# Seven-product form in more weight groups of a two-layer attention and recurrence trunk on one Trainium2 core, with the weight sums added by DMA

## What is computed

```python
for l in range(DEPTH):
    h = _rmsnorm(x, norm_gain[l])
    proj = jnp.einsum('bsd,de->bse', h, w_in[l])
    q, k, v, g_attn, x_rnn, g_rnn = jnp.split(proj, splits, axis=-1)
    attn = _swa_sink_attention(q, k, v, sinks[l], cos, sin)
    xc = _causal_conv(x_rnn, conv_w[l], conv_b[l])
    rnn = _rg_lru(xc, w_rgate[l], b_rgate[l], w_igate[l], b_igate[l], lru_param[l])
    mixed = jnp.concatenate([attn * jax.nn.silu(g_attn), rnn * jax.nn.silu(g_rnn)], axis=-1)
    x = x + jnp.einsum('bse,ed->bsd', mixed, w_out[l])
return _rmsnorm(x, final_gain)
```

## Time and profile before

| | us |
|---|---|
| median of 3 runs | 2312.78 (2311.39 to 2314.31) |
| the profiled execution | 2313.38 |
| its span in the profile | 2311.6 |
| PE busy | 2296.4 (99%) |
| DVE busy | 1637.6 (71%) |
| ACT busy | 1330.1 (58%) |
| read from memory | 244.48 MB |

### The profile page before, as it was taken

The page is one execution under the profiler, slowest core; times in us unless marked ns, Lnnn a source line. Parts: engine busy times, 40 slices in busy tenths (PEclk is TensorE's granted clock), DMA queues, the critical chain, the costliest instruction groups (busy, mean ns, idle before and its releaser), DMA issues.

```text
span 2311.6 us, 36747 instructions
## 1 busy us (share of the span) xinstructions
PE 2296.4 (99%) x13690; PEld 1915.2 (83%) x13690; DVE 1637.6 (71%) x2767; ACT 1330.1 (58%) x2551; POOL 0.8 (0%) x10
## 2 busy tenths in 40 slices
PE   9999999999999999999999999999999999999999
PEld 8888888898888888888888888888888888888888
DVE  7568778766547877867675786787765478777775
ACT  7558666434456767644565676763354557666444
POOL 0000000000000000000000000000000000000000
PEclk9999999999999999999999999999999999999999
DMA  5334333434333233344435433233343333333344
GB/s 194 103 109 139 95 89 92 117 113 123 95 99 88 85 99 85 99 143 117 148 96 157 164 105 93 89 97 115 116 119 97 95 95 89 89 90 100 110 119 151
DMA packets 138563, 255.28 MB, mean 110 GB/s; under 512 B 15632, under 2 KB 30224, under 8 KB 137616
## 3 DMA queue, kind: packets, MB, share of 16 engines
q1 hardware_dynamic: 137808, 252.77, 36.6%
q10 hardware_dynamic: 576, 0.16, 0.0%
HBM read 244.48 MB, written 8.39 MB: 109 GB/s over the span
## 4 chain that ended last, share of the span: by engine, by line
PE 85%; DVE 8%; DMA 4%; issue 2%; ACT 2%; SPq 0%; DVEq 0%; ACTq 0%; POOL 0%; POOLq 0%
PE proj L508 75%; DMA wraw<-in_w 3%; PE proj L527 2%; DVE wcut L1140 2%; PE proj L541 2%; PE ps_at L621 1%; PE ps_at L646 1%; PE ps_at L665 1%; PE proj L557 1%; DVE x L1443 1%; ACT wcut L750 1%; DVE room L1154 1%; DVE wraw L1155 1%; DVE wraw L1156 1%; DVE room L1158 0%
## 5 line engine op out<-in xcount | busy, mean ns | idle before, releaser
L508 PE MATMUL proj<-operand,wcut 128*128 128x512 f32 x8520 | 1973.2, 391 | 0.3 <-DVE proj L1203 0.3
L508 PEld LDWEIGHTS proj<-operand,wcut 128*128 128x128 f32 x8520 | 1591.4, 188 | 343.9 <-issue 11.2
L750 ACT ACTIVATE wcut<-wraw 128x512 fp32r<-128x512 f32 x803 | 505.6, 630 | 768.4 <-PE proj L508 657.3
L1140 DVE TENSOR_TENSOR wcut<-wraw,wcut 128x512 fp32r<-128x512 f32 x804 | 553.6, 689 | 522.5 <-ACT wcut L750 517.7
L527 PE MATMUL proj<-xsum,wcut 128*128 128x256 f32 x720 | 99.4, 283 | 0.0
L527 PEld LDWEIGHTS proj<-xsum,wcut 128*128 128x128 f32 x720 | 92.1, 192 | 0.0
L907 ACT ACTIVATE room<-ps_at,stat 128x128 f32<-128x128 f32 x256 | 90.0, 363 | 0.8
L855 ACT ACTIVATE gy<-proj 32x512 f32<-32x512 f32 x144 | 85.0, 590 | 3.8
L760 ACT ACTIVATE crosscut<-room 128x384 fp32r<-128x384 f32 x80 | 42.0, 526 | 54.5 <-DMA room<-in_w 26.5
L541 PE MATMUL proj<-operand,crosscut 128*128 128x256 f32 x480 | 70.5, 283 | 0.0
L541 PEld LDWEIGHTS proj<-operand,crosscut 128*128 128x128 f32 x480 | 64.3, 192 | 1.2
(11 more groups left out here) (181 smaller groups left out, 1810.0 us busy)
## 6 DMA issues: line engine op xcount, KB each, us to landing
wraw<-in_w SPq DMA_DIRECT2D x804, 256.0 KB, 2.6
room<-in_w SPq DMA_DIRECT2D x80, 128.0 KB, 2.7
x<-in_xt SPq DMA_DIRECT2D x2, 4096.0 KB, 13.7
mixed<-in_xt SPq DMA_DIRECT2D x14, 512.0 KB, 7.1
gw<-in_gates SPq DMA_DIRECT2D x32, 128.0 KB, 2.7
out<-x SPq DMA_DIRECT2D x4, 1024.0 KB, 4.9
out<-mixed SPq DMA_DIRECT2D x7, 512.0 KB, 3.2
tab<-in_cossin SPq DMA_DIRECT2D x8, 256.0 KB, 3.5
```

The source lines that it names most:

```text
L508: last = pe.matmul(bank[:, :], wcut[:, u % RING, a, c:c + P], operand[:, k, b, :], start=(k == 0 and n == 0), stop=(k == KT - 1 and n == 2 ...
L750: act.activation(wcut[:, u % RING, 0, :], wraw[:, u % RING, :], ACT.Copy).then_inc(w_hi, 1)
L1140: dve.tensor_tensor(wcut[:, u % RING, 1, :], wraw[:, u % RING, :], wcut[:, u % RING, 0, :].bitcast(F32), ALU.subtract).then_inc(w_lo, 1)
```

## The change

The seven-product form is used in more groups: 12 to 15 of the input projection and 19 to 24 of the output projection in every pass (19 to 23 in the last), and 4 to 6 in the passes of layer 2. That is 10, 13, 10 and 12 groups in the four passes, where 5 in each were before.

The order of the products is new. A group in this form has four whole units and seven half units: each half unit is one of the seven products for all four pairs (12 matmuls of 256 columns), with a weight tile of 256 KB of its own. Four of them (`lead`) run in the slots of the group before, three (`late`) in the group's own slots. `beats_of` says which units a slot holds: none, one or two. ACT and DVE cut the tile of a slot's first unit at its start and that of the second at its end. The wait for the banks' evacuation stands before the last matmul of the unit ahead.

The weight sums S1 to S4 are made by POOL's DMAs in device memory, copies and accumulating transfers from a second copy of the weights (`blocks`), 12 batches of one or two groups, during the first half of the tokens; the second half reads them again. `weight_sums`, `cross_part` and `crosscut` are gone.

The token sums of the input projection are computed by DVE into the room of `x`. For that, `x` is stored to device memory in slots 1 to 4 of layer 2 (four transfers of 1 MB), and in both layers it is loaded again at slot 125 (`RELOAD`), after the last half unit of group 15; the reload at slot 60 is gone. In layer 1 the output stores free the room.

Queries are evacuated at 0 and 2 slots after their group, and the second tile of an xr group after 2 slots instead of 6. The tables' second load moves from slot 196 to 70, the identity's load to the end.

```diff
+IN_LAST = 15
+EARLY_SEVEN = {(0, 0): (), (0, 1): (4, 5, 6), (1, 0): (), (1, 1): (4, 5, 6)}
+SEVEN = {(h, l): (*EARLY_SEVEN[h, l], *range(12, IN_LAST + 1),
+                  *range(PG + 2, PG + (7 if (h, l) == (LAST, DEPTH - 1) else 8)))
+         for h in range(HALVES) for l in range(DEPTH)}
+NPAIR = 4
+JS = {"in": (0, 1, 4, 5), "out": (0, 1, 2, 3)}
+LEAD = ((0, 0, 0, None), (1, 0, 1, 1), (3, 1, 1, 0), (2, 1, 0, 2))
+LATE_OF = ((4, 0, 0, None), (5, 0, 1, None), (6, 1, 0, 3))
+A11, S2, S3, S1, A12, S4, A22, A21 = range(8)
+WHOLE = {A11: 0, A12: 1, A21: 2, A22: 3}
+SUMS = {S1: 0, S3: 1, S2: 2, S4: 3}
...
+def beats_of(h, l, g):
+    mine, ahead = g in SEVEN[h, l], g + 1 in SEVEN[h, l]
+    p = [("plain", g, j) for j in range(UPG) if not mine or j not in JS[zone_of(g)]]
+    a = [("lead", g + 1, b) for b in range(4)]
+    t = [("late", g, b) for b in range(3)]
+    if mine and ahead:
+        return [t[:2], p[:1], p[1:2], t[2:], a[:2], a[2:], p[2:3], p[3:]]
+    if mine:
+        return [t[:1], t[1:2], p[:1], t[2:], p[1:2], [], p[2:3], p[3:]]
+    if ahead:
+        return [p[:1], p[1:2], p[2:3], [p[3], a[0]], [p[4], a[1]], [p[5], a[2]], a[3:], p[6:]]
+    return [[n] for n in p]
...
-Q_EV = 16
+Q_AT = [2 * UPG + UPG * (t // 2) + 2 * (t % 2) for t in range(AT)]
...
-XR_EV = [slot_of("xr", j) + 6 * (j % 2) for j in range(RT)]
+XR_EV = [slot_of("xr", j) + 2 * (j % 2) for j in range(RT)]
...
-TAB_LD = 196
+TAB_LD = 70
+T_AT = {(h, l, "out"): (126, 128, 136, 143) for h in range(HALVES) for l in range(DEPTH)}
+T_AT.update({(0, 0, "in"): (24, 26, 28, 30), (0, 1, "in"): (6, 7, 9, 11), (1, 0, "in"): (25, 33, 41, 49),
+             (1, 1, "in"): (6, 7, 9, 11)})
+SPILL = (1, 3, 0, 2)
+SPILL_AT = 1
+RELOAD = UPG * IN_LAST + 5
...
+                        for u in BEAT[h, l, s]:
+                            next_u = u + RING if u + RING < TOTAL else u + RING - UPG
+                            kind, g, j = UNIT[next_u][2:]
+                            what = {"lead": LEAD, "late": LATE_OF}[kind][j][0] if kind != "plain" else None
+                            sp_.wait_ge(w_lo, u + 1)
+                            if h == 0 and what in SUMS:
+                                sp_.wait_ge(built[what], 32 * (batch_of(UNIT[next_u][1], g) + 1))
+                            sp_.dma_start(wraw[:, u % RING, :], source(next_u)).then_inc(w_in[u % RING], 16)
...
+                        if l == 1 and s - SPILL_AT in range(4):
+                            i = SPILL[s - SPILL_AT]
+                            sp_.wait_ge(evac, at_evac(h, 0, tile_of("o", 4 * i + 3)))
+                            sp_.dma_start(x_kept[i], x[:, 4 * i:4 * i + 4, :].rearrange("p k t -> p (k t)")
+                                          ).then_inc(kept[i], 16)
+                        if s == RELOAD:
+                            sp_.wait_ge(unit_done, TURNED[h, l, "in"])
+                            if l == 0:
+                                sp_.dma_start(x[:, :, :], xt[h]).then_inc(xres_in, 16)
+                            else:
+                                sp_.dma_start(x[:, :, :].rearrange("p (i k) t -> p i (k t)", i=4),
+                                              x_kept.rearrange("i p c -> p i c")).then_inc(xres_in, 16)
...
+            def copy(to, batch, what):
+                l, g, size = BATCH[batch]
+                src = (blocks[WHOLE[what], l, g:g + size] if what in WHOLE else sums[SUMS[what], l, g:g + size])
+                pool.dma_start(sums[SUMS[to], l, g:g + size].rearrange("g r e -> (g r) e"),
+                               src.rearrange("g r e -> (g r) e")).then_inc(built[to], 16)
+            def add(to, batch, what):
+                l, g, size = BATCH[batch]
+                pool.dma_start(sums[SUMS[to], l, g:g + size].rearrange("g r e -> (g r) e"),
+                               blocks[WHOLE[what], l, g:g + size].rearrange("g r e -> (g r) e"),
+                               accum_op=ALU.add, max_dma_last_dim=4 * 4 * TOK).then_inc(built[to], 16)
+            pool.wait_ge(unit_done, START_SUMS)
+            for n in range(len(BATCH) + 1):
+                now, before = n < len(BATCH), n > 0
+                if before:
+                    copy(S4, n - 1, S2)
+                if now:
+                    copy(S1, n, A21)
+                    copy(S3, n, A11)
+                    pool.wait_ge(built[S1], 32 * n + 16)
+                    add(S1, n, A22)
+                    pool.wait_ge(built[S3], 32 * n + 16)
+                    add(S3, n, A21)
+                if before:
+                    pool.wait_ge(built[S4], 32 * n - 16)
+                    add(S4, n - 1, A12)
+                if now:
+                    pool.wait_ge(built[S3], 32 * n + 32)
+                    copy(S2, n, S3)
+                    pool.wait_ge(built[S2], 32 * n + 16)
+                    add(S2, n, A22)
+                    pool.wait_ge(built[S2], 32 * n + 32)
+                    pool.wait_ge(built[S1], 32 * n + 32)
+                if before:
+                    pool.wait_ge(built[S4], 32 * n)
...
+            def next_bank(n):
+                h, l, kind, g, j = UNIT[n]
+                if n > 0 and UNIT[n - 1][:2] == (h, l) and j == 0 and (kind == "lead" or (kind == "plain" and
+                                                                                     g not in SEVEN[h, l])):
+                    pe.wait_ge(evac, h * (DEPTH * TILES) + (l * TILES + 2 * g + 2))
...
+            def halved(n):
+                h, l, kind, g, j = UNIT[n]
+                zone = zone_of(g)
+                what, m, half, t = (LEAD if kind == "lead" else LATE_OF)[j]
+                if t is not None and g == next(i for i in SEVEN[h, l] if zone_of(i) == zone):
+                    pe.wait_ge(xsum_lo, at_t(h, l, zone, NPAIR - 1))
+                for i, pair in enumerate(JS[zone]):
+                    for p, (a, b) in enumerate(((0, 0), (0, 1), (1, 0))):
+                        if t is None:
+                            src = operand[:, KU * pair + (kind == "late"), b, HT * half:HT * half + HT]
+                        else:
+                            src = xsum[zone][i][:, HI_PART[zone][i] ^ b, t, :]
+                        if (i, p) == (NPAIR - 1, 2):
+                            next_bank(n + 1)
+                        last = pe.matmul(bank_of(l, 2 * g + m)[:, HT * half:HT * half + HT],
+                                         wcut[:, n % RING, a, P * i:P * i + P], src,
+                                         start=(kind == "lead" and j % 2 == 0 and (i, p) == (0, 0)),
+                                         stop=(kind == "lead" and (i, p) == (NPAIR - 1, 2)), skip_group_check=True)
...
+                act.activation(lead_u[:, :], bank_of(l, 2 * g)[:, 0:HT], ACT.Copy).then_inc(lead_copy, 1)
+            def lead_copy_back(h, l, g):
+                n = LED.index((h, l, g))
+                act.wait_ge(lead_done, 3 * n + 3)
+                act.activation(bank_of(l, 2 * g + 1)[:, 0:HT], lead_v[:, :], ACT.Copy).then_inc(lead_back, 1)
...
-            def weight_sums(h, l, g, i):
...
+                    mark(dve.tensor_tensor(to[0], first[:, 0:HT], first[:, HT:TOK], ALU.subtract))
+                    mark(dve.tensor_scalar(to[0], to[0], g1, None, ALU.mult))
+                    mark(dve.scalar_tensor_tensor(to[1], second[:, HT:TOK], g2, to[0], ALU.mult, ALU.add))
+                    mark(dve.scalar_tensor_tensor(to[2], first[:, 0:HT], g1, to[1], ALU.mult, ALU.subtract))
+                    dve.scalar_tensor_tensor(to[3], second[:, 0:HT], g2, to[1], ALU.mult,
+                                             ALU.subtract).then_inc(xsum_done, 1)
...
+                dve.wait_ge(unit_done, LED_AT[3][n])
+                dve.wait_ge(lead_half, n + 1)
+                if n > 0:
+                    dve.wait_ge(lead_back, n)
+                dve.tensor_tensor(first[:, HT:TOK], second[:, HT:TOK], lead_u[:, :], ALU.add).then_inc(lead_done, 1)
+                dve.tensor_tensor(lead_v[:, :], second[:, 0:HT], lead_u[:, :], ALU.subtract).then_inc(lead_done, 1)
+                dve.wait_ge(lead_done, 3 * n + 2)
+                dve.tensor_tensor(second[:, HT:TOK], lead_v[:, :], second[:, HT:TOK], ALU.subtract).then_inc(lead_done, 1)
...
+                        for u in BEAT[h, l, s][1:]:
+                            if u + AHEAD < TOTAL:
+                                weight_lo(u + AHEAD)
+                                dve.wait_ge(w_lo, u + AHEAD + 1)
```

474 lines of the change are left out of this document (231 added, 243 removed).

## The result

The change makes the kernel slower: 2374.74 us (2365.05 to 2376.78, four runs) against 2313.55 us, a ratio of 1.0257 with a 95% interval of 1.0242 to 1.0272. The profiled execution has a span of 2375.0 us, 63.4 us more than before's 2311.6. The forecast of 2350 had the sign and the main mechanism, but 24.7 us too little, and the time lies 2.7 us above the range. The four executions took 2376.8, 2376.8, 2372.7 and 2365.1 us, at mean granted clocks of PE of 0.989, 0.990, 0.992 and 0.995; before's are within 3 us of each other. The profiled one is the slowest of the four.

A forecast was written before the change was run, and what follows sets the result against it. PE's matmul stream, busy 99%, and its waits bound the kernel. Terms -20.4 - 9 + 19.5 + 5.4 + 18.6 + 4.6 + 18.8 = +37.5 us on a median of 2312.8 gave 2350 us, range 2290 to 2372.

The forecast's parts named there:

- Pitches and columns: All seven-product groups: matmuls stay at 227 and 120 ns, 0.816 us less per group, -20.4 us for 25 more groups.
- Lead starts in the output projection: Output projection: leads no longer wait for DVE's residual addition, -9 us (bounds -7.5 and -11.8).
- Passages: Block 24 into layer 2: DVE's last residuals end after the next layer's second unit is due, +4.6 us; next half nothing.
- Lead against evacuation: Layer 2, groups 4 to 6: leads wait for query evacuation, +19.5 us; block 6's gate matmul waits, +5.4 us.
- Blocks 12 to 14: Input projection, all passes: DVE falls behind with added tiles and lead sums, 4 x 4.65 = +18.6 us.
- Reload: Slot 125, all passes: a weight tile lands late behind the 4 MB of x, PE waits, 4 x 4.7 = +18.8 us.
- the rival in which it stays hidden: Reload of x: tiles do not queue behind it or block 16 absorbs it, total 2331 us, chance 0.17.
- Weight sums by DMA: POOL's 12 batches: fifth due near 518 us, 98 us a batch available, so taken at 0.
- Token sums: Input projection: 14 us a pass on DVE, spread over slots well under 2.72 us, so 0 (up to 2 per pass).
- The cover holds: Rival: ACT and DVE enter slot 3 a slot earlier, stalls vanish, only -29.4 remains, 2283 us, chance 0.16.
- half of it: Rival: each place costs half, near 2317 us (2300 to 2320), chance 0.10.
- DMA sums late: Rival: with steps over 25 us PE waits for layer 1's last batches of weight sums, over 2372 us, chance 0.07.

The follow-up runs named there:

- The output form alone: Seven-product form only in the output projection, x loaded in four 1 MB parts, weight sums after slot 72, against the kernel before: 2305.48 us, ratio 0.9968.
- experiment 3: Changed kernel with leads, and ACT's and DVE's sums of them, one slot later where one seven-product group follows another: 2360.73 us, ratio 1.0203 to before.
- the kernel with groups 14 and 15 alone: Seven-product form in groups 14, 15 and the output projection, x in four parts, stores two slots later, against the kernel before: 2303.88 us, ratio 0.9961.

## Why the forecast was right and where it was not

**Which steps failed.** The time fell outside the range because three things that cost time stood at nothing in the sum: what the weight sums' transfers do to the tiles beside them (11.1 us), what the token sums do to a store that the change leaves alone (5.2 us), and the clock behind a stop of PE (9.6 us in layer 2's blocks 3 to 6, 1.6 in block 12 of the third pass, and parts of the 11.1 and the 5.2). The terms that had waits priced in them came out within 2.0 us each, the clock left out.

**Pitches and columns: right.** Blocks 19 to 22 take 21.0 us each in all passes; 48 x 227 + 84 x 120 ns is 20.98. By the 518 and 262 cycles of the Trainium skill's page "TensorE: Matmul & The Clock Gate", section "Back-to-back issue gap", a group would take 19.5 us, an estimate; the blocks here are against it.

**Lead starts in the output projection: right, -10.6 against -9,** inside the bounds of -7.5 and -11.8. The output form alone moves the time by 2305.48 - 2312.71 = -7.2 us, and the span by -8.1. Three more groups make -2.4 of it, the passages +4.1 and the lead starts -10.6, together -8.9; 0.8 of the span's step is not assigned.

**Passages: 4.1 against 4.6, and not all where they were put.** The two passages to layer 2 cost 1.7 each, where 2.3 was forecast; the one to the next half costs 0.8, where nothing was.

**Lead against evacuation: the waits right to 0.6 us each, the clock behind them left out.** The forecast let PE come to block 5's lead 9.64 us into the block and the second query leave at 15.45, a wait of 5.8. The timeline of the changed kernel, whose block starts at 716.9:

```profile
727.52 2.43 ACT L962 ACTIVATE gy<-proj 32x512 f32<-32x512 f32 x4 [0.96 <-DVE q L1446]
...
731.96 0.68 DVE L1389 TENSOR_TENSOR gy<-gy,tab 128x512 f32<-128x512 f32 x1
...
732.70 0.58 PE L651 MATMUL proj<-xsum_in,wcut 128*128 128x256 f32 x1 [6.01 <-DVE gy L1389]
```

The query leaves at 732.64, 15.7 us into the block, and PE waits 6.0. Block 4's wait is 3.2 against 2.75, the gate's in block 6 2.2 against 2.7, block 3's 1.4 against 1.15. The waits make 2 x 12.8 = 25.6 us, where 24.9 were forecast, and at a clock of 1.00 the four blocks would stand 26.9 us over their time without waits. The other 9.6 us of the measured 36.5 are the clock: the forecast kept 2.4 GHz throughout because every window of the kernel before shows 1.00, and never asked what the row would be after a stop of PE of a kind that the kernel before doesn't have.

**Blocks 12 to 14: right, 18.3 against 18.6.** Block 12 costs 3.1 (4.7 in the third pass, with 1.6 from the clock), block 13 nothing, block 14 1.1, in each pass. The forecast gave block 12 3.6, so the clock makes up for a wait put too high. DVE's lateness was the reason given, and experiment 3 bears it out: moving the leads only moves the wait. In the kernel with groups 14 and 15 alone block 14 again costs 1.1 and block 13 nothing.

**Reload: right, 18.0 against 18.8,** and the rival in which it stays hidden falls. In the first pass the clock has a part in it too (0.94 in block 16, where the waits of PE are 2.8 us and the block costs 5.1). The row of before that was nearest (a tile landing in 11.6 us behind the 4 MB) was the right one to go by.

**Weight sums by DMA: wrong, 0 against 11.1 (6.4 of it standstill of PE, the rest with the clock).** The step that failed asked only whether the sums are ready in time. They are: the fifth batch was due near 518 us, and all run from 27 to about 370 us at some 28 us a batch. It did not ask what they do to the weight tiles meanwhile, though before's trace shows a 4 MB load raising a tile's landing to 11.6 us. The cost appears almost only in stretches with little cover: 11.1 us in blocks 12 to 14, 15 in the output blocks, 10.3 beside a 4 MB load, nothing in blocks 1 to 10 of layer 2; beside whole units it was 1.6 us, in block 9 of the first pass of three kernels. By the Trainium skill's page "DMA: Bandwidth & Descriptors", section "Anatomy of one DMA", a step was estimated at 3.2 us; the landing here is 6.4 us (accumulating transfers and first copies together) and 5.1 us (copies of a sum), so the runs do not agree with it for these transfers from memory to memory.

**Token sums: wrong, 0 against 5.2 at one place (3.6 of it the wait, 1.6 the clock).** DVE was said to stand well under 2.72 us a slot. True on average; around slots 41 to 44 of the third pass it has softmax, a query, a token sum and the scaling of the output, and behind it SP's queue. "Other queues: 0" considered only the DMAs that the change moves, not those that stay and wait for an engine made later.

**Rivals.** "The cover holds" and "half of it" are excluded; the first needed block 5 of layer 2 to reach 9.6 us without a wait. "DMA sums late" gave the right region of time for a wrong reason: nothing waits for a sum.

**What stays open.** Blocks with the same waits differ by 1.6 us between passes and executions (block 12: 26.9 or 28.5), and the granted clock tells them apart. Why it falls behind the waits of one pass and not behind the same waits of another, no run here tells, so a forecast could have given this cost a range, but no single number.

## What to carry to other kernels

Half the columns for 53% of the price also halve the time that the buffers ahead can cover: a form that saves 0.8 us a group pays only where no other engine is near its limit (here the output projection, and by the blocks groups 14 and 15), and one wait of 6 us eats seven groups. A wait of PE can cost more than it lasts: ask what the clock does behind it, also when the kernel before shows 1.00 everywhere. Ask of a background transfer not only when it is ready but which runs with little cover it passes beside, split a long load that shares a queue with tiles, and put it beside the work with the most cover. When a wait is added, look at every queue whose entries wait for the engine that gets later, also at those entries that the change leaves alone.

## What the hardware showed that I had not expected

**The clock falls behind a stop.** After PE's wait of 6.0 us the granted clock is 0.50 in the next 6 us window; matmuls whose result nobody reads, run in that wait and in the one of 3.2 us in block 4, keep it at 1.00 there, and layer 2's blocks 3 to 6 are 7.9 us shorter in two passes. It can also fall where no wait is that long: block 12, whose longest is 1.4 us, has it at 0.94 in the third pass and takes 1.6 us more. The whole kernel before shows 1.00, so its trace gives no hint of it.

**A clock below 1.00 need not cost time.** Where the leads are later, block 12 takes 27.0 us with a stretch at 0.50 in it and 27.0 without one. And the kernel with the reload in four parts was profiled with a mean clock of 0.942, near 0.95 in most stretches, also where PE is busy throughout:

```profile
500.00:520.00 20.00, 20.00 (x126) 18.08 (x125) 11.44 (x19) 8.16 (x14) 0.00 (x0) 0.95 0.51 145
```

Its output blocks take the same 21.0 us. Why, no run here tells; a level of 0.95 in these records is not to be turned into time.

**Memory to memory.** Copying one sum of 512 KB to another took 5.1 us to land; the group that holds the accumulating transfers, and the first copies with them, took 6.4 us. Beside them, in blocks 12 to 14 of the first pass, the median landing of a 256 KB tile rose from 2.7 to 3.9 us and the longest from 5.2 to 10.5.
